# Other places in SBUF for the split weights where they are the stationary operand

## The chip, the cores and the metric

One core of a Trainium2 chip runs the whole program. The metric is the device time of one execution in microseconds; the time of before is the median of three runs.

## What is computed

Two decoder layers over 256 tokens of width 2048, float32. Layer 0 mixes tokens with block attention (16 heads of 128, one block of 256 tokens, so plain causal attention), layer 1 with retention (8 heads, keys of 256, values of 512). Behind each stands a gated feed-forward part with a causal convolution of width 3 (hidden width 5632), and every residual sum is followed by a layer norm. Cut to the two parts that carry most of the weights:

```python
qkv = jnp.einsum('bsd,de->bse', x, w_qkv)            # 2048 -> 3*2048, attention
# retention: w_q, w_k (2048 -> 2048), w_v, w_g (2048 -> 4096), w_o (4096 -> 2048)
def conv_ffn(x, w_in, conv_w, conv_b, w_out):
    u = jnp.einsum('bsd,df->bsf', x, w_in)           # 2048 -> 2*5632
    up = jnp.pad(u, ((0, 0), (CONV_WIDTH - 1, 0), (0, 0)))
    c = conv_b + up[:, 0:S] * conv_w[0]
    for j in range(1, CONV_WIDTH):
        c = c + up[:, j:j + S] * conv_w[j]
    g, val = jnp.split(c, 2, axis=-1)
    return jnp.einsum('bsf,fd->bsd', jax.nn.gelu(g) * val, w_out)
h = layer_norm(DEEPNORM_ALPHA * h + m, ln_g[i, 0], ln_b[i, 0])
```

## The kernel before

All weights, 478 MB, pass through the core once as 912 chunks. A chunk is 256 rows by 512 columns of a weight matrix: 128 partitions with CK = 2 row blocks of 512 float32 (COLS). There is a ring of RING = 4 slots. For each chunk SyncE loads `raw[:, s]` (512 KB), ScalarE rounds it into the high part `w_hi[:, s]` (float32r, `round_chunk`, recorded at L507), VectorE puts raw minus high into the low part `w_lo[:, s]` (`split_chunk`, L727), and TensorE multiplies. Each product of float32 values is made of three float32r products: high by high, high by low, low by high. The semaphores `hi_ready`, `lo_ready` and `products` hand a chunk on from engine to engine and a slot back; SyncE reloads `raw` of a slot once `lo_ready` says that the difference is made, ScalarE and VectorE overwrite the parts once `products` says that TensorE has finished with them. ScalarE and VectorE go through the chunks in `stream`, which takes other steps of a stage (`slots` ahead of a chunk, `behind` after it). `stream` for chunk s of a product prepares the chunk four further on, which for the last four belongs to the next product.

TensorE multiplies a chunk in one of three ways:
- token-major (`multiply_tile`, L272, L274, L275): 128x128 of the activations is stationary, a row block of 512 weight columns moves; the sum has tokens on the partitions. 12 matmuls a chunk. Used for values, gates and all output projections.
- feature-major narrow (`multiply` with `feature_major`, L289, L291, L293): 128x128 of the weights is stationary, 256 tokens of `x_hi` or `x_lo` move. 24 matmuls a chunk. Used for queries and keys.
- feature-major wide (`wide_multiply`, L330, L333): 128x128 of `w_hi` is stationary for 512 columns, the `x_hi` and `x_lo` of one row block side by side; then 128x128 of `w_lo` for the 256 columns of `x_hi`. 16 matmuls a chunk. Used for the input weights of the feed-forward part.

Every matmul loads its own stationary operand. The loads and matmuls of TensorE follow one another with no wait between them but that for `lo_ready` once a chunk. The order of stages is attention (narrow, narrow, token-major per group of four heads), its output, feed-forward 0 (wide, then token-major), retention (narrow, token-major, token-major per head), its output, feed-forward 1.

In SBUF each of h, x_parts, raw, w_hi and w_lo takes a multiple of 2048 bytes per partition, one after the other. Small tensors follow, and a padding "align" of 128 bytes, then arena (which holds the outputs of attention, retention and the hidden values, high and low, under other names) and side.

The lines that lay out the ring's parts are

```python
        raw = sb("raw", [P, RING, CK, COLS])
        w_hi = sb("w_hi", [P, RING, CK, COLS], F32R)
        w_lo = sb("w_lo", [P, RING, CK, COLS], F32R)
```

Of the kernel before, what the change touches and what calls it, by code (L numbers as in the profile page):

```python
# [22 lines left out]
F32 = mybir.dt.float32  # L23
# [12 lines left out]
CK = 2  # L36
RING = 4
# [22 lines left out]
HOLD = 2  # L60
AHEAD = 4
# [46 lines left out]
def build_trunk(nc, x, weights, attn_tab, causal, ident_in, ret_tab, decay_tab, conv_in, ln_g, ln_b, out):  # L108
    with ExitStack() as ctx:
# [11 lines left out]
        w_hi = sb("w_hi", [P, RING, CK, COLS], F32R)  # L121
        w_lo = sb("w_lo", [P, RING, CK, COLS], F32R)
# [55 lines left out]
        acc_a, acc_b, acc_c, mid = acc_ab[:, 0:2], acc_ab[:, 2:4], acc_cm[:, 0:2], acc_cm[:, 2:4]  # L178

# [85 lines left out]
        def _(pe):  # L265
            def multiply_tile(acc, t, s, xh, xl, kt, first):
# [3 lines left out]
                wh, wl = w_hi[:, s % RING], w_lo[:, s % RING]  # L270
# [234 lines left out]
        def _(act):  # L505
# [3 lines left out]
            def round_chunk(turn, s):  # L509
                act.wait_ge(raw_in[s], 16 * turn + 16)  # L510
                copy(w_hi[:, s], raw[:, s]).then_inc(hi_ready, 1)

            def stream(turn, chunks, slots={}, behind={}):


                for s in range(chunks):
# [4 lines left out]
                    round_chunk(turn + s // RING + 1, s % RING)  # L521
# [16 lines left out]
            for p in range(AHEAD):  # L538
                round_x(0, p)
                if p < RING:  # L540
                    round_chunk(0, p)
# [22 lines left out]
            def group(g):  # L564
                turn = Q_ATTN_LOOP + 3 * XQ * g
                stream(turn, XCH)
                stream(turn + XQ, XCH, {
# [16 lines left out]
            stream(Q_ATTN, XCH, behind=merged(x_slots(0), {1: [load_tables]}))  # L584
            with act.Fori(0, GROUPS - 1) as g:
                tail = group(g)
                stream(Q_ATTN_LOOP + 2 * XQ + 3 * XQ * g, XCH, tail)
            tail = group(GROUPS - 1)
# [3 lines left out]
            for n in range(1, NBLK):  # L592
                stream(Q_WO + n * XQ, XCH)
# [15 lines left out]
            def ffn(layer, q_in, n_in, nc_in, q_out, last):  # L609
# [25 lines left out]
                def behind_value(i):  # L635
# [3 lines left out]
                       behind=x_slots(2 * layer + 1))  # L639
                with act.Fori(0, FSTEPS - 1) as i:  # L640
                    turn = q_in + XQ + 2 * XQ * i
                    stream(turn, XCH, value_block(i))
                    stream(turn + XQ, XCH, merged(behind_value(i), {
                        XCH - 1: [lambda: conv_first_part(acc_ab)]}))
                stream(q_out - XQ, XCH, value_block(FSTEPS - 1))
# [5 lines left out]
                for i in range(NBLK // 2):  # L651
                    slots = merged(behind_value(FSTEPS - 1), {4: [load_behind_hidden]}) if i == 0 else {}

                    stream(q_out + OQ * i, 2 * HCH - (RING if last and i == NBLK // 2 - 1 else 0), slots)
# [20 lines left out]
            def retention_head(hd):  # L675
                turn = Q_RET_LOOP + 3 * XQ * hd
                stream(turn, XCH, {XCH - 1: [lambda: values_copy(rv_sb, acc_b, b_free)]})
                stream(turn + XQ, XCH, {XCH - 1: [make_gate]})
                return {1: [lambda: round_y(hd)]}

            stream(Q_RET, XCH, behind=merged(x_slots(2), {PIECES - AHEAD: [load_ret_tables]}))
            with act.Fori(0, RHEADS - 1) as hd:
                tail = retention_head(hd)
                stream(Q_RET_LOOP + 2 * XQ + 3 * XQ * hd, XCH, tail)
            tail = retention_head(RHEADS - 1)
            stream(Q_RWO, RCH, tail)
            load_ln_params(3)
            for n in range(1, NBLK):
                stream(Q_RWO + n * RQ, RCH)
# [34 lines left out]
        def _(dve):  # L724
            def split_chunk(turn, s):
                dve.wait_ge(hi_ready, RING * turn + (s + 1))
                dve.tensor_tensor(w_lo[:, s], raw[:, s], w_hi[:, s].bitcast(F32), ALU.subtract).then_inc(lo_ready, 1)  # L727

            def stream(turn, chunks, slots={}, at=0, behind={}):


                for s in range(chunks):
# [3 lines left out]
                    split_chunk(turn + (at + s) // RING + 1, (at + s) % RING)  # L736
# [9 lines left out]
            for p in range(AHEAD):  # L746
                low_x(0, p)
                if p < RING:
                    split_chunk(0, p)
# [47 lines left out]
            def group(g):  # L797
# [356 lines left out]
```

## Time and profile before

| | |
|---|---|
| median of 3 runs | 2656.99 us (2656.34 to 2658.08) |
| profiled execution | 2648.49 us |
| its span, first to last instruction | 2646.7 us |
| mean granted TensorE clock | 0.995 |
| busy: TensorE, its weight loads, VectorE, ScalarE, GpSimd | 2612.0, 2266.8, 1600.4, 1257.2, 15.2 us |

Times are microseconds from the start of the span, unless marked ns. PE is TensorE's matmuls, PEld its weight loads, DVE VectorE, ACT ScalarE, POOL GpSimd, SP SyncE. L12 is line 12 of the kernel. A matmul's record lasts from its start to the modelled end of its pipeline, so neighbours overlap; the pace is read from the starts. Some matmul records are missing from a trace. A float32 matmul (not float32r) has two records.

### The profile page before, as it was taken

Reading aid. Unit: us, or ns where it says so; the run is one execution under the profiler, and the core shown is the slowest. Engines: PE = TensorE matmul, PEld = TensorE weight load, DVE = VectorE, ACT = ScalarE, POOL = GpSimd, SP = SyncE. Lnnn points to the kernel's source line nnn. Section 1 sums busy time; section 2 is a strip of 40 time slices with the busy share of each in tenths; the row PEclk is TensorE's granted clock in tenths of the full one; section 3 lists DMA queues with packets and bytes.
Section 4 is the critical chain, followed back from the end, with each engine's and each line's share of the span. In section 5 each row is a group of like instructions: output and inputs, shape, how many; then the busy total and the mean of one; then the engine's idle time right before and its main releaser. Section 6 shows DMA issues by size and latency. Waiting matters only on the chain.

```text
span 2646.7 us, 40802 instructions
## 1 busy us (share of the span) xinstructions
PE 2612.0 (99%) x14368; PEld 2266.8 (86%) x14368; DVE 1600.4 (60%) x1842; ACT 1257.2 (48%) x1387; POOL 15.2 (1%) x38
## 2 busy tenths in 40 slices
PE   8999999999999999999999999999999999999998
PEld 8999888888888888888888888888788888888886
DVE  5666657666666654475555555554666666665455
ACT  4444435565656443334444444343365656554332
POOL 0000000000000000000000000000000000000000
PEclk9999999999999999999999999999999999999999
DMA  6545564555555565655555555566455555556654
GB/s 221 175 163 171 174 223 158 191 189 188 188 188 189 204 216 192 192 177 175 169 182 177 175 177 174 178 222 197 155 188 190 186 194 183 194 190 228 196 188 148
DMA packets 136978, 493.78 MB, mean 187 GB/s; under 512 B 15056, under 2 KB 17104, under 8 KB 135888
## 3 DMA queue, kind: packets, MB, share of 16 engines
q1 hardware_dynamic: 133136, 481.49, 55.1%
q10 hardware_dynamic: 3776, 11.37, 1.2%
q8 instruction: 46, 0.75, 0.1%
q14 instruction: 20, 0.16, 0.0%
HBM read 490.70 MB, written 2.10 MB: 186 GB/s over the span
## 4 chain that ended last, share of the span: by engine, by line
PE 98%; DVE 1%; DMA 0%; POOL 0%; issue 0%; ACT 0%; DVEq 0%; POOLq 0%; ACTq 0%
PE acc_ab L330 12%; PE acc_cm L330 12%; PE acc_ab L272 11%; PE acc_ab L274 11%; PE acc_ab L275 11%; PE acc_ab L333 6%; PE acc_cm L333 6%; PE acc_ab L289 5%; PE acc_ab L291 5%; PE acc_ab L293 5%; PE acc_cm L272 3%; PE acc_cm L275 3%; PE acc_cm L274 3%; PE acc_cm L356 1%; PE acc_cm L460 0%; DVE h L847 0%
## 5 line engine op out<-in xcount | busy, mean ns | idle before, releaser
L727 DVE TENSOR_TENSOR w_lo<-raw,w_hi 128x1024 fp32r<-128x1024 f32 x912 | 1105.8, 1223 | 838.2 <-ACT w_hi L507 835.2
L507 ACT ACTIVATE w_hi<-raw 128x1024 fp32r<-128x1024 f32 x912 | 948.7, 1055 | 882.7 <-PE acc_ab L275 469.7
L330 PE MATMUL acc_ab<-x_parts,w_hi 128*128 128x512 f32 x1408 | 493.7, 396 | 0.0
L330 PE MATMUL acc_cm<-x_parts,w_hi 128*128 128x512 f32 x1408 | 489.1, 394 | 0.0
L333 PE MATMUL acc_ab<-x_parts,w_lo 128*128 128x256 f32 x1408 | 391.4, 278 | 0.0
L333 PE MATMUL acc_cm<-x_parts,w_lo 128*128 128x256 f32 x1408 | 390.0, 277 | 0.0
L330 PEld LDWEIGHTS acc_ab<-x_parts,w_hi 128*128 128x128 f32 x1408 | 265.5, 189 | 61.3
L330 PEld LDWEIGHTS acc_cm<-x_parts,w_hi 128*128 128x128 f32 x1408 | 264.0, 188 | 61.3
L289 PE MATMUL acc_ab<-x_parts,w_hi 128*128 128x256 f32 x1024 | 295.8, 289 | 2.1 <-DVE w_lo L727 2.1
L291 PE MATMUL acc_ab<-x_parts,w_hi 128*128 128x256 f32 x1024 | 291.6, 285 | 0.0
L293 PE MATMUL acc_ab<-x_parts,w_lo 128*128 128x256 f32 x1024 | 291.6, 285 | 0.0
L272 PE MATMUL acc_ab<-w_hi,hid_hi 128*128 128x512 f32 x704 | 274.1, 389 | 0.0
L275 PE MATMUL acc_ab<-w_hi,hid_lo 128*128 128x512 f32 x704 | 273.9, 389 | 0.0
L274 PE MATMUL acc_ab<-w_lo,hid_hi 128*128 128x512 f32 x704 | 273.9, 389 | 0.0
L333 PEld LDWEIGHTS acc_ab<-x_parts,w_lo 128*128 128x128 f32 x1408 | 265.7, 189 | 0.0
L333 PEld LDWEIGHTS acc_cm<-x_parts,w_lo 128*128 128x128 f32 x1408 | 264.3, 188 | 0.0
L289 PEld LDWEIGHTS acc_ab<-x_parts,w_hi 128*128 128x128 f32 x1024 | 198.5, 194 | 2.9 <-issue 2.5
L291 PEld LDWEIGHTS acc_ab<-x_parts,w_hi 128*128 128x128 f32 x1024 | 198.5, 194 | 0.4
L293 PEld LDWEIGHTS acc_ab<-x_parts,w_lo 128*128 128x128 f32 x1024 | 198.3, 194 | 0.0
L272 PEld LDWEIGHTS acc_ab<-w_hi,hid_hi 128*128 128x128 f32 x704 | 132.1, 188 | 27.9 <-DVE w_lo L727 0.4
L274 PEld LDWEIGHTS acc_ab<-w_lo,hid_hi 128*128 128x128 f32 x704 | 132.1, 188 | 27.4
L275 PEld LDWEIGHTS acc_ab<-w_hi,hid_lo 128*128 128x128 f32 x704 | 132.1, 188 | 27.4
(111 smaller groups left out, 2839.2 us busy)
## 6 DMA issues: line engine op xcount, KB each, us to landing
raw<-in_weights_dram SPq DMA_DIRECT2D x912, 512.0 KB, 4.0
ln_gain<-in_ln_g_dram ACTq DMA_DIRECT2D x4, 1024.0 KB, 7.8
ln_bias<-in_ln_b_dram ACTq DMA_DIRECT2D x4, 1024.0 KB, 11.3
h<-in_x_dram SPq DMA_DIRECT2D x4, 512.0 KB, 8.4
decay_sb<-in_decay_tab_dram ACTq DMA_DIRECT2D x1, 1024.0 KB, 6.9
out_dram<-h SPq DMA_DIRECT2D x4, 256.0 KB, 2.5
out_dram<-h ACTq DMA_DIRECT2D x3, 256.0 KB, 2.5
conv_par<-in_conv_in_dram ACTq DMA_DIRECT2D x1, 352.0 KB, 11.4
```

Of the source, the lines that this page charges most:

```text
L272: pe.matmul(o, xh[:, kt + k, c], wh[:, k], start=first and k == 0, stop=False, skip_group_check=True)
L274: pe.matmul(o, xh[:, kt + k, c], wl[:, k], start=False, stop=False, skip_group_check=True)
L275: done = pe.matmul(o, xl[:, kt + k, c], wh[:, k], start=False, stop=True, skip_group_check=True)
L289: pe.matmul(o, wh[:, k, c], xh[:, kt + k, :], start=first and k == 0 and f % 2 == 0, stop=False, skip_group_check=True)
L291: pe.matmul(o, wh[:, k, c], xl[:, kt + k, :], start=False, stop=False, skip_group_check=True)
L293: last = pe.matmul(o, wl[:, k, c], xh[:, kt + k, :], start=False, stop=True, skip_group_check=True)
L330: pe.matmul(acc[:, f], w_hi[:, s % RING, k, c], x_parts[:, CK * s + k].rearrange("p a n -> p (a n)"), start=s == 0 and k == 0, stop=False, ...
L333: last = pe.matmul(acc[:, f, SEQ:2 * SEQ], w_lo[:, s % RING, k, c], x_hi[:, CK * s + k, :], start=False, stop=True, skip_group_check=True)
L356: last = pe.transpose(x_bank(p)[:, f, t * P:(t + 1) * P], h[:, t, p * PIECE + f * P:p * PIECE + (f + 1) * P], ident[:])
L507: return act.activation(o, i, ACT.Copy)
L727: dve.tensor_tensor(w_lo[:, s], raw[:, s], w_hi[:, s].bitcast(F32), ALU.subtract).then_inc(lo_ready, 1)
```

## The change

The parts of a slot get 64 floats more (256 bytes): `w_hi` and `w_lo` become [P, RING, SLOT] with SLOT = CHUNK + 64 and CHUNK = CK * COLS = 1024. A chunk's high and low part begin at a place within the slot: TOKENS = (0, 0) for the token-major products, FEATURES = (32, 48) floats for both feature-major ones, so at 128 bytes in w_hi and 192 bytes in w_lo. `parts(s, place)` makes the views. TensorE takes them by the kind of product, ScalarE and VectorE by two new arguments of `stream`: `place` for the chunks that belong to the running product and `then` for the four that belong to the next. Which values are computed, in which order and with which waits doesn't change. What lies behind w_hi in SBUF moves up by 1024 bytes, and what lies behind w_lo by 2048.

```diff
+CHUNK = CK * COLS
+TOKENS, FEATURES = (0, 0), (32, 48)
+SLOT = CHUNK + 64
...
-        w_hi = sb("w_hi", [P, RING, CK, COLS], F32R)
-        w_lo = sb("w_lo", [P, RING, CK, COLS], F32R)
+        w_hi = sb("w_hi", [P, RING, SLOT], F32R)
+        w_lo = sb("w_lo", [P, RING, SLOT], F32R)
...
+        def parts(s, place):
+
+            return [w[:, s, at:at + CHUNK].rearrange("p (k n) -> p k n", k=CK)
+                    for w, at in zip((w_hi, w_lo), place)]
...
-                wh, wl = w_hi[:, s % RING], w_lo[:, s % RING]
+                wh, wl = parts(s % RING, TOKENS)
...
-                wh, wl = w_hi[:, s % RING], w_lo[:, s % RING]
                 if feature_major:
+                    wh, wl = parts(s % RING, FEATURES)
...
+                wh, wl = parts(s % RING, FEATURES)
                 for k in range(CK):
                     for f in range(4):
                         c = slice(f * P, (f + 1) * P)
-                        pe.matmul(acc[:, f], w_hi[:, s % RING, k, c],
+                        pe.matmul(acc[:, f], wh[:, k, c],
                                   x_parts[:, CK * s + k].rearrange("p a n -> p (a n)"),
                                   start=s == 0 and k == 0, stop=False, skip_group_check=True)
-                        last = pe.matmul(acc[:, f, SEQ:2 * SEQ], w_lo[:, s % RING, k, c], x_hi[:, CK * s + k, :],
+                        last = pe.matmul(acc[:, f, SEQ:2 * SEQ], wl[:, k, c], x_hi[:, CK * s + k, :],
                                          start=False, stop=True, skip_group_check=True)
...
-            def round_chunk(turn, s):
+            def round_chunk(turn, s, place):
                 act.wait_ge(raw_in[s], 16 * turn + 16)
-                copy(w_hi[:, s], raw[:, s]).then_inc(hi_ready, 1)
-
-            def stream(turn, chunks, slots={}, behind={}):
+                copy(parts(s, place)[0], raw[:, s]).then_inc(hi_ready, 1)
+
+            def stream(turn, chunks, slots={}, behind={}, place=TOKENS, then=TOKENS):
...
-                    round_chunk(turn + s // RING + 1, s % RING)
+                    round_chunk(turn + s // RING + 1, s % RING, place if s + RING < chunks else then)
...
-            def split_chunk(turn, s):
+            def split_chunk(turn, s, place):
                 dve.wait_ge(hi_ready, RING * turn + (s + 1))
-                dve.tensor_tensor(w_lo[:, s], raw[:, s], w_hi[:, s].bitcast(F32), ALU.subtract).then_inc(lo_ready, 1)
+                wh, wl = parts(s, place)
+                dve.tensor_tensor(wl, raw[:, s], wh.bitcast(F32), ALU.subtract).then_inc(lo_ready, 1)
```

The rest of the diff hands `place` and `then` to each call of `stream`.

## Rows read from the trace of the kernel before

**Rows 1.** The page's busy time by engine, with share of the span and instructions.
```profile
PE 2612.0 (99%) x14368; PEld 2266.8 (86%) x14368; DVE 1600.4 (60%) x1842; ACT 1257.2 (48%) x1387; POOL 15.2 (1%) x38
```
**Rows 2.** The page's chain that ended last, share of the span by engine.
```profile
PE 98%; DVE 1%; DMA 0%; POOL 0%; issue 0%; ACT 0%; DVEq 0%; POOLq 0%; ACTq 0%
```
**Rows 3.** The waits of TensorE: who for whom, us in total, times, longest.
```profile
PE acc_cm L356 <- DVE h L855: 13.7, 6, 3.5
PE acc_cm L356 <- DMA h<-in_x_dram: 5.7, 1, 5.7
PE acc_ab L289 <- DVE w_lo L727: 2.1, 1, 2.1
PE acc_ab L272 <- DVE o_lo L794: 1.1, 1, 1.1
```
**Rows 4.** Timeline of a narrow product on TensorE: start, duration, instruction.
```profile
50.01 0.28 PE L293 MATMUL acc_ab<-x_parts,w_lo 128*128 128x256 f32 x1
...
51.09 0.28 PE L293 MATMUL acc_ab<-x_parts,w_lo 128*128 128x256 f32 x1
```
**Rows 5.** Timeline of a wide product on TensorE, f = 0 first.
```profile
500.51 0.39 PE L330 MATMUL acc_ab<-x_parts,w_hi 128*128 128x512 f32 x1
500.74 0.27 PE L333 MATMUL acc_ab<-x_parts,w_lo 128*128 128x256 f32 x1
500.85 0.40 PE L330 MATMUL acc_ab<-x_parts,w_hi 128*128 128x512 f32 x1
501.08 0.28 PE L333 MATMUL acc_ab<-x_parts,w_lo 128*128 128x256 f32 x1
501.20 0.39 PE L330 MATMUL acc_ab<-x_parts,w_hi 128*128 128x512 f32 x1
...
503.28 0.39 PE L330 MATMUL acc_ab<-x_parts,w_hi 128*128 128x512 f32 x1
...
506.06 0.39 PE L330 MATMUL acc_ab<-x_parts,w_hi 128*128 128x512 f32 x1
```
**Rows 6.** Timeline of a token-major product on TensorE.
```profile
999.90 0.39 PE L275 MATMUL acc_ab<-w_hi,hid_lo 128*128 128x512 f32 x1
...
1001.49 0.39 PE L272 MATMUL acc_ab<-w_hi,hid_hi 128*128 128x512 f32 x1
```
**Rows 7.** The page's groups: xcount | busy, mean ns | idle before.
```profile
L727 DVE TENSOR_TENSOR w_lo<-raw,w_hi 128x1024 fp32r<-128x1024 f32 x912 | 1105.8, 1223 | 838.2 <-ACT w_hi L507 835.2
L507 ACT ACTIVATE w_hi<-raw 128x1024 fp32r<-128x1024 f32 x912 | 948.7, 1055 | 882.7 <-PE acc_ab L275 469.7
L330 PE MATMUL acc_ab<-x_parts,w_hi 128*128 128x512 f32 x1408 | 493.7, 396 | 0.0
L289 PE MATMUL acc_ab<-x_parts,w_hi 128*128 128x256 f32 x1024 | 295.8, 289 | 2.1 <-DVE w_lo L727 2.1
L272 PE MATMUL acc_ab<-w_hi,hid_hi 128*128 128x512 f32 x704 | 274.1, 389 | 0.0
```
**Rows 8.** Stretches: length, busy by engine, clock, DMA share, GB/s.
```profile
8.00:50.00 42.00, 40.21 (x320) 40.24 (x321) 27.66 (x27) 19.14 (x23) 0.00 (x0) 1.00 0.68 236
430.00:890.00 460.00, 460.00 (x2655) 402.31 (x2654) 310.53 (x375) 275.11 (x313) 0.00 (x0) 1.00 0.57 189
900.00:1120.00 220.00, 220.00 (x971) 181.85 (x970) 112.42 (x104) 89.46 (x87) 0.00 (x0) 1.00 0.62 202
...
2400.00:2630.00 230.00, 230.00 (x1016) 190.39 (x1015) 116.26 (x108) 89.58 (x85) 0.00 (x0) 1.00 0.59 194
```
**Rows 9.** The chain in order of time around float32 products: start, us.
```profile
1199.94 0.86 PE acc_cm L468 x2
...
1227.33 0.87 PE acc_cm L478 x8
```
**Rows 10.** The wide 256-column matmuls, 500 to 560: ns min/median/max.
```profile
L333 PE MATMUL acc_cm<-x_parts,w_lo x66: 274/277/280, 500.0 to 544.8; 128*128 128x256 f32 x66
```
**Rows 11.** The page's DMA issues: KB each, us to landing.
```profile
raw<-in_weights_dram SPq DMA_DIRECT2D x912, 512.0 KB, 4.0
```

More of the change, by code:

```diff
@@ L540, in _ @@
                 if p < RING:
-                    round_chunk(0, p)
+                    round_chunk(0, p, FEATURES)
             def head_exp(g, i):
@@ L562, in head_round, with group @@
                 copy(o_hi[:, bass.ds(hd, 1), :], mid[:, 1:2, 0:SEQ]).then_inc(o_hi_done, 1)
-            def group(g):
+            def group(g, then):
                 turn = Q_ATTN_LOOP + 3 * XQ * g
-                stream(turn, XCH)
-                stream(turn + XQ, XCH, {
+                stream(turn, XCH, place=FEATURES, then=TOKENS)
+                stream(turn + XQ, XCH, then=then, slots={
                     3: [lambda: head_exp(g, 0)],
@@ L592, in _ @@
             for n in range(1, NBLK):
-                stream(Q_WO + n * XQ, XCH)
+                stream(Q_WO + n * XQ, XCH, then=FEATURES if n == NBLK - 1 else TOKENS)
             def conv_first_part(acc):
@@ L652, in ffn @@
                     slots = merged(behind_value(FSTEPS - 1), {4: [load_behind_hidden]}) if i == 0 else {}
-                    stream(q_out + OQ * i, 2 * HCH - (RING if last and i == NBLK // 2 - 1 else 0), slots)
+                    stream(q_out + OQ * i, 2 * HCH - (RING if last and i == NBLK // 2 - 1 else 0), slots,
+                           then=FEATURES if i == NBLK // 2 - 1 and not last else TOKENS)
             ffn(0, Q_FFN0, N_FFN0, NC_FFN0, Q_OUT0, False)
@@ L688, in _ @@
             for n in range(1, NBLK):
-                stream(Q_RWO + n * RQ, RCH)
+                stream(Q_RWO + n * RQ, RCH, then=FEATURES if n == NBLK - 1 else TOKENS)
             ffn(1, Q_FFN1, N_FFN1, NC_FFN1, Q_OUT1, True)
@@ L724, in _, with stream @@
         def _(dve):
-            def split_chunk(turn, s):
+            def split_chunk(turn, s, place):
                 dve.wait_ge(hi_ready, RING * turn + (s + 1))
-                dve.tensor_tensor(w_lo[:, s], raw[:, s], w_hi[:, s].bitcast(F32), ALU.subtract).then_inc(lo_ready, 1)
-            def stream(turn, chunks, slots={}, at=0, behind={}):
+                wh, wl = parts(s, place)
+                dve.tensor_tensor(wl, raw[:, s], wh.bitcast(F32), ALU.subtract).then_inc(lo_ready, 1)
+            def stream(turn, chunks, slots={}, at=0, behind={}, place=TOKENS, then=TOKENS, last=None):
                 for s in range(chunks):
@@ L735, in stream @@
                         step()
-                    split_chunk(turn + (at + s) // RING + 1, (at + s) % RING)
+                    split_chunk(turn + (at + s) // RING + 1, (at + s) % RING,
+                                place if s + RING < (last or chunks) else then)
                     for step in behind.get(s, ()):
@@ L795, in head_low, with group @@
                                   o_hi[:, bass.ds(hd, 1), :].bitcast(F32), ALU.subtract).then_inc(o_ready, 1)
-            def group(g):
+            def group(g, then):
                 turn = Q_ATTN_LOOP + 3 * XQ * g
                 stream(turn, XCH, {
-                    XCH - 1: [lambda: rotate(2 * g + 1, acc_b, b_free, g, k_t)]})
-                stream(turn + XQ, XCH, {
+                    XCH - 1: [lambda: rotate(2 * g + 1, acc_b, b_free, g, k_t)]}, place=FEATURES, then=TOKENS)
+                stream(turn + XQ, XCH, then=then, slots={
                     3: [lambda: head_max(g, 0)],
@@ L924, in _ @@
                     lambda: residual(1, n, (acc_a, acc_b)[n % 2], (a_free, b_free)[n % 2], N_WO + n // 2)]})
-            stream(Q_FFN0 - XQ, XCH - HOLD)
+            stream(Q_FFN0 - XQ, XCH - HOLD, last=XCH, then=FEATURES)
             layer_norm(1)
@@ L991, in ffn @@
                     else:
-                        stream(turn, HCH - (RING if last else HOLD), at=HCH)
+                        stream(turn, HCH - (RING if last else HOLD), at=HCH, last=HCH, then=TOKENS if last else FEATURES)
                 if last:
@@ L1053, in low_y, with retention_head @@
                                   ALU.subtract).then_inc(y_ready, 1)
-            def retention_head(hd):
+            def retention_head(hd, then):
                 turn = Q_RET_LOOP + 3 * XQ * hd
@@ L1074, in _ @@
                                      (N_RWO, NB_RWO)[n % 2] + n // 2)]})
-            stream(Q_FFN1 - RQ, RCH - HOLD)
+            stream(Q_FFN1 - RQ, RCH - HOLD, last=RCH, then=FEATURES)
             layer_norm(3)
```

59 lines of the change are left out of this document (30 added, 29 removed).

## The prediction, written before the changed kernel was run

> **What bounds the kernel now.** I read the engine table first, then the chain that ended last, then what TensorE waited for, and only then single matmuls. TensorE is busy 99% of the span, VectorE 60%, ScalarE 48% [rows 1]. The chain is 98% TensorE [rows 2], and all of TensorE's idle time is 22.6 us in nine waits, for the layer norms and the start [rows 3]. So nothing but the pace of the matmuls matters here, and a change that only moves operands can act on the path only through that pace.
>
> The pace comes from the distance between the starts of neighbouring matmuls; the durations in the group rows overlap and don't add up. Three kinds of product stream the chunks of weights:
> - narrow (L289, L291, L293), weights stationary, 256 moving columns: starts at 50.01 and 51.09 with nine steps between, 120.0 ns each [rows 4];
> - wide (L330, L333), weights stationary, a pair of 512 and 256 moving columns per place: 500.51 to 506.06 is 16 pairs (eight to a chunk, whose next chunk begins at 503.28), 346.9 ns a pair [rows 5];
> - token-major (L272, L274, L275), x, o, y or the hidden values stationary, 512 columns of weights moving: 999.90 to 1001.49 is seven steps, 227.1 ns each [rows 6].
>
> The counts are 1024 of each of three narrow lines (8 to a chunk, so 128 chunks) and 1408 in each of two accumulators for each wide line (2816 pairs, 352 chunks); of the 912 chunks 432 are left for the token-major products, 5184 matmuls at 12 each [rows 7]. Then 3072 x 120.0 = 369 us, 2816 x 346.9 = 977 us, 5184 x 227.1 = 1177 us: 2523 of the span of 2646.7. The rest is float32 products, transposes and the waits.
>
> Now the columns. The granted clock reads 1.00 in the stretches of every kind [rows 8], so a column takes 1/2.4 = 0.417 ns if one enters per cycle. 256 columns are 106.7 ns, and 13.3 are left over; a wide pair is 320.0, and 26.9 are left over, 13.4 for each of its two matmuls; 512 columns are 213.3, and 13.8 are left over. So **each matmul with its own load of 128 x 128 weights pays about 32 cycles extra**, whether it has 256 or 512 columns and whichever operand is stationary. That extra is the only thing this change can reach.
>
> Is it a fixed fee? The float32 products speak against. Two records of L468 with 512 columns take 0.86 us on the chain, 430 ns each: two cycles per column (426.7) and 3.3 left over. Eight transposes of 128 columns (L478) take 0.87: 108.8 ns each, two cycles per column (106.7) and 2.1 left over [rows 9]. They too load 128 x 128 float32 weights before each matmul. So a load every 109 ns can be nearly free when the moving operand is read at half the pace. That looks like two reads of SBUF in each other's way, which is what the place of an operand could change. It isn't proof: those records are another kind of pass.
>
> **Where the operands lie.** Before the change the rows of x_parts, raw, w_hi and w_lo take a multiple of 2048 bytes each. Between w_lo and arena lie 3968 bytes of small tensors (each at a multiple of 32) and the 128 of "align", together 4096. So the start of every operand of the three products has the same remainder modulo 512, and TensorE never ran them at another relative place. No row of before shows what 128 or 192 bytes do. There is one hint. Of the wide pairs the one with f even takes 0.34 us from start to start and the one with f odd 0.35, over and over; the 256-column matmul, which streams the same x_hi both times, takes 274 or 280 ns [rows 5, 10], where the weights stand 512 bytes further and the sum goes to the next PSUM bank. Between the starts it is 0.11 against 0.12. I read some 5 ns from it: the place of an operand can move a matmul by that much. The PSUM bank could be its cause as well.
>
> **The change part by part.**
> 1. Weights stationary, w_hi at 128 and w_lo at 192 bytes: 3072 narrow and 5632 wide loads, 8704 in all, on the path. Upper end of the gain: the extra falls from 13.4 to the 2.1 of the transposes, 11.3 x 8704 = 98 us. Lower end: nothing, and beyond it a loss, since a common start may just as well be the good place; doubling the extra would be 13.4 x 8704 = +117 us, which no row comes near. I take the size that the nearest row shows for an address, 5 ns a load, as a gain: 5 x 8704 = **43.5 us**. I choose the sign because the extra is at its full size everywhere while all operands share one start, and goes where reads are slower; a start at another place is then likelier to help than to hurt.
> 2. Weights moving: same places within a slot, but slots are 4352 bytes apart, so slot s starts 256 s further, modulo 1024. 5184 matmuls; slot 0 is as before. Cost nothing if 256 bytes don't matter; if they cost the same 5 ns in three slots of four, 5 x 3888 = 19 us either way. I take 0: in a wide chunk steps of 512 and 1024 bytes only trade 5 ns to and fro, and the two halves of the moving x_parts, 1024 bytes apart, both give 120 ns [rows 4].
> 3. ScalarE's copy and VectorE's difference write and read the shifted parts: the same 912 of each, 1055 and 1223 ns [rows 7]. No instruction or transfer is added or moved; SyncE's and ScalarE's queues are as before. A slower one is covered: in the wide stretch VectorE works 310.5 of 460 us and ScalarE 275.1 [rows 8], with 166 chunks in it; a chunk would need 0.9 us more VectorE time before it became late. Without that cover each microsecond per chunk in the 480 shifted chunks (128 narrow, 352 wide) would be on the path.
> 4. What is late next if the matmuls speed up: a wide chunk takes 2.775 us; all of the extra gone, 16 x 11.3 = 0.18 less, 2.59. Then 512 KB per chunk ask for 202 GB/s instead of 189. Another stretch moved 202 GB/s and the first 236, with TensorE busy throughout the one and nearly so in the other [rows 8]; the load lands after 4.0 us and three other slots cover it [rows 11]. So the gain is kept.
>
> The Trainium skill speaks against step 1. Its page "SBUF — State Buffer", section "Who interferes with whom", gives TensorE two independent read ports, for the moving operand and for the weights, and says TensorE never waits for anyone. By it the sum would be 0; the extra of 13.4 ns shows a fee that it doesn't name, and the trace can't tell whether that fee depends on the place. The same page, section "Specifications (TRN2)", gives lines of 16 bytes: a load's 512 bytes per partition are 32 lines, the number of extra cycles. If each line cost one cycle and the new places avoided it, the sum would be the upper end.
>
> Sum: 2646.7 - 43.5 = 2603.2 span, 2605.0 for the profiled execution (2648.5, 1.8 outside the span). That execution is 8.5 below the median of the runs, 2657.0, so the forecast is 2657.0 - 43.5 = **2613.5 us**.
>
> **The rivals.**
> - All of the extra goes: 2657 - 98 = 2559. For: 32 cycles are left at every place alike, and almost none in float32. Against: w_hi and w_lo get different shifts, while one stream is often a whole row of 2048 bytes, which sweeps every place of a smaller period whatever the start.
> - The place doesn't matter: 2657. For: the extra is the same 32 cycles for 256 and 512 columns and for either operand stationary, as a fixed fee of swapping weights would be; the 5 ns may be the PSUM bank. The two ports of the Trainium skill, as told above, would give the same.
> - The common start is the good one, and a shifted load meets the moving rows more often. Place: the same 8704 loads; price 5 ns each, +43.5, and up to 19 more in the token-major products: 2700 to 2720. It decides as soon as a narrow matmul takes over 120 ns. For: the padding "align" brings arena to the same remainder as w_hi, and there the pace is no worse than elsewhere. Against: nothing shows that pace to be below that of another start.
>
> **How the numbers follow.** Forecast, part of the extra goes (2585 to 2651): 0.45. All or nearly all goes (2556 to 2585): 0.14. No effect: 0.22. Slower: 0.19. A measurement of this kernel tells about 0.2% (5.3 us) from no change. Faster 0.59, same 0.22, slower 0.19. The range leaves out the slower case alone: 2557 to 2662.
>
> **What would show it.** Right: L289, L291 and L293 start less than 120 ns apart (115 for the forecast, 109 for all of it), wide pairs below 347 (337, 324), the token-major ones stay at 227, as do TensorE's waits of 22.6 us. If narrow and wide go different ways, the price per load is wrong, since I use one for both. If the token-major matmuls move, step 2 is wrong. If ScalarE or VectorE take the time back, TensorE waits for w_lo appear. If all starts are where they were, the fee is fixed.

## The result and the profile after

| | before | after |
|---|---|---|
| median | 2656.97 us (2656.34 to 2658.08, 4 executions) | 2640.66 us (2640.04 to 2642.14, 4 executions) |
| ratio, 95% interval | | 0.995 (0.9931 to 0.997) |
| profiled execution, its span | 2648.49, 2646.7 us | 2640.04, 2638.2 us |

The change makes the kernel 16.3 us (0.6%) faster in the medians. The forecast was 43.5 us. The profiled executions differ by 8.5 us only, and that difference between the two differences is half of the story. One execution of narrow_only further down had a mean granted clock of 0.556, where all others had 0.994 to 0.996; it took 4385 us and is left out of its row.

The page of after has, by engine and by chain, what [rows 1, 2] have for before:

```profile
PE 2603.5 (99%) x14368; PEld 2265.8 (86%) x14368; DVE 1600.7 (61%) x1842; ACT 1258.8 (48%) x1387; POOL 15.2 (1%) x38
PE 98%; DVE 1%; DMA 0%; POOL 0%; issue 0%; ACT 0%; DVEq 0%; POOLq 0%; ACTq 0%
```

Its waits of TensorE are the same nine as in [rows 3], 22.7 us against 22.6:

```profile
PE acc_cm L367 <- DVE h L869: 13.7, 6, 3.5
PE acc_cm L367 <- DMA h<-in_x_dram: 5.8, 1, 5.8
PE acc_ab L299 <- DVE w_lo L740: 2.1, 1, 2.1
PE acc_ab L282 <- DVE o_lo L808: 1.1, 1, 1.1
```

So the time went from the pace of the matmuls and from nothing else. The groups of VectorE and ScalarE, which write the shifted parts, hardly differ from [rows 7] (xcount | busy, mean ns | idle before):

```profile
L740 DVE TENSOR_TENSOR w_lo<-raw,w_hi 128x1024 fp32r<-128x1024 f32 x912 | 1106.1, 1223 | 832.2 <-ACT w_hi L518 823.7
L518 ACT ACTIVATE w_hi<-raw 128x1024 fp32r<-128x1024 f32 x912 | 950.1, 1057 | 874.3 <-PE acc_ab L285 468.9
```

Now the three kinds of product, in the timeline of TensorE (start, duration, instruction). First narrow, to hold against [rows 4]:

```profile
49.59 0.28 PE L303 MATMUL acc_ab<-x_parts,w_lo 128*128 128x256 f32 x1
...
50.99 0.28 PE L303 MATMUL acc_ab<-x_parts,w_lo 128*128 128x256 f32 x1
```

Twelve steps in 1.40 us: 116.7 ns each, where before had 120.0. Then wide, against [rows 5]:

```profile
500.47 0.39 PE L341 MATMUL acc_ab<-x_parts,w_hi 128*128 128x512 f32 x1
500.70 0.28 PE L344 MATMUL acc_ab<-x_parts,w_lo 128*128 128x256 f32 x1
500.81 0.39 PE L341 MATMUL acc_ab<-x_parts,w_hi 128*128 128x512 f32 x1
...
506.01 0.39 PE L341 MATMUL acc_ab<-x_parts,w_hi 128*128 128x512 f32 x1
```

Sixteen pairs in 5.54 us, 346.3 ns a pair; before had 346.9. Chunk by chunk it is the same number in both traces: the last matmuls of neighbouring wide chunks lie 2773 or 2774 ns apart in all 169 places of a layer where no other matmul lies between, in both layers, before and after. And token-major, against [rows 6]:

```profile
1000.09 0.39 PE L282 MATMUL acc_ab<-w_hi,hid_hi 128*128 128x512 f32 x1
...
1000.77 0.39 PE L282 MATMUL acc_ab<-w_hi,hid_hi 128*128 128x512 f32 x1
...
1001.45 0.39 PE L282 MATMUL acc_ab<-w_hi,hid_hi 128*128 128x512 f32 x1
```

Six steps in 1.36 us, 226.7 ns each: unchanged.

A steady chunk takes 2880, 2800, 2773.3 or 2720 ns here, and in cycles of 2.4 GHz (the granted clock is 1.00 in these windows) these figures turn out whole. A chunk of 24 narrow matmuls had 32.0 extra cycles per matmul before and has 24.0 after; a wide chunk of 16 has 32.0 in both; a token-major one of 12 has 32.0 in both. From here on I give the pace as **extra cycles per matmul**, the chunk's time times 2.4, less its columns, divided by its matmuls. They are taken from the starts of the last matmul of each chunk, the median over the chunks of a stage that hold no other matmul. At some places the chunks take turns between two or three lengths; the median then lies up to half a cycle off the mean (40.4 further down is 40.0 in the mean).

### The profile page after: what moved, and what is told of

Same layout as the page of the kernel before. It is cut to its first block, busy times and chain, and to the rows that moved or that the text cites. A ratio compares the mean times of both kernels' runs of the same rounds, so it can differ in the third digit from the quotient of the medians.

```text
span 2638.2 us, 40802 instructions
## 1 busy us (share of the span) xinstructions
PE 2603.5 (99%) x14368; PEld 2265.8 (86%) x14368; DVE 1600.7 (61%) x1842; ACT 1258.8 (48%) x1387; POOL 15.2 (1%) x38
## 4 chain that ended last, share of the span: by engine, by line
PE 98%; DVE 1%; DMA 0%; POOL 0%; issue 0%; ACT 0%; DVEq 0%; POOLq 0%; ACTq 0%
PE acc_ab L341 12%; PE acc_cm L341 12%; PE acc_ab L282 11%; PE acc_ab L284 11%; PE acc_ab L285 11%; PE acc_ab L344 6%; PE acc_cm L344 6%; PE acc_ab L299 5%; PE acc_ab L303 5%; PE acc_ab L301 5%; PE acc_cm L282 3%; PE acc_cm L285 3%; PE acc_cm L284 3%; PE acc_cm L367 1%; PE acc_cm L471 0%; DVE h L861 0%
## 5 line engine op out<-in xcount | busy, mean ns | idle before, releaser
L740 DVE TENSOR_TENSOR w_lo<-raw,w_hi 128x1024 fp32r<-128x1024 f32 x912 | 1106.1, 1223 | 832.2 <-ACT w_hi L518 823.7
L518 ACT ACTIVATE w_hi<-raw 128x1024 fp32r<-128x1024 f32 x912 | 950.1, 1057 | 874.3 <-PE acc_ab L285 468.9
L341 PEld LDWEIGHTS acc_ab<-x_parts,w_hi 128*128 128x128 f32 x1408 | 265.7, 189 | 57.9
L299 PE MATMUL acc_ab<-x_parts,w_hi 128*128 128x256 f32 x1024 | 293.1, 286 | 2.1 <-DVE w_lo L740 2.1
L301 PE MATMUL acc_ab<-x_parts,w_hi 128*128 128x256 f32 x1024 | 286.4, 280 | 0.0
L299 PEld LDWEIGHTS acc_ab<-x_parts,w_hi 128*128 128x128 f32 x1024 | 194.5, 190 | 2.9 <-issue 2.5
L301 PEld LDWEIGHTS acc_ab<-x_parts,w_hi 128*128 128x128 f32 x1024 | 194.7, 190 | 0.5
```

The lines of the kernel that those rows point to most:

```text
L299: pe.matmul(o, wh[:, k, c], xh[:, kt + k, :], start=first and k == 0 and f % 2 == 0, stop=False, skip_group_check=True)
L301: pe.matmul(o, wh[:, k, c], xl[:, kt + k, :], start=False, stop=False, skip_group_check=True)
L341: pe.matmul(acc[:, f], wh[:, k, c], x_parts[:, CK * s + k].rearrange("p a n -> p (a n)"), start=s == 0 and k == 0, stop=False, skip_group_ ...
L518: return act.activation(o, i, ACT.Copy)
L740: dve.tensor_tensor(wl, raw[:, s], wh.bitcast(F32), ALU.subtract).then_inc(lo_ready, 1)
```

## The experiments

The kernels of the scans give each stage its own places. For them the changed kernel was written so that `place` and `then` are handed down by stage, with one pair of floats each for the narrow, wide and token-major products of attention, retention and the two feed-forward layers. The other kernels of this section except after_again are written in the same way. Only the constants differ between them (x_moved has two lines more, shown there); those of scan4 are, in floats, with layer 0 and layer 1 in brackets:

```diff
-TOKENS, FEATURES = (0, 0), (32, 48)
+ATTN_NARROW, ATTN_TOKEN, FFN_WIDE, FFN_TOKEN = (16, 48), (48, 16), [(16, 32), (16, 48)], [(48, 32), (0, 8)]
+RET_NARROW, RET_TOKEN = (32, 0), (48, 48)
```

Places are given in bytes, w_hi first; "0 and 0" is the start of the slot. Nothing is left out of the computation in any of them.

### The changed kernel again, its slots alone, and its narrow half

after_again is the changed kernel. stride_only keeps the wider slots and begins all parts at their start:

```diff
-TOKENS, FEATURES = (0, 0), (32, 48)
+ATTN_NARROW, ATTN_TOKEN, FFN_WIDE, FFN_TOKEN = (0, 0), (0, 0), [(0, 0), (0, 0)], [(0, 0), (0, 0)]
+RET_NARROW, RET_TOKEN = (0, 0), (0, 0)
```

narrow_only keeps (32, 48) in the narrow products and (0, 0) in the wide ones:

```diff
-TOKENS, FEATURES = (0, 0), (32, 48)
+ATTN_NARROW, ATTN_TOKEN, FFN_WIDE, FFN_TOKEN = (32, 48), (0, 0), [(0, 0), (0, 0)], [(0, 0), (0, 0)]
+RET_NARROW, RET_TOKEN = (32, 48), (0, 0)
```

> The changed kernel once more, timed in five rounds beside the kernel before. In its trace the narrow matmuls start 116.7 ns apart instead of 120.0 and the wide pairs are as before, 346.7 ns. Theory A (the place of the stationary weights sets the pace of the narrow products alone): a chunk of 24 narrow matmuls takes 2.80 us instead of 2.88, over 128 chunks 10 us, so the median is 8 to 11 us below before and not 16. Theory B (the wide products gain too, which one profile hides): 15 to 18 us below before.

> Slots are 4352 bytes apart as in the changed kernel, and everything behind them lies where it lies there, but all parts begin at the start of their slots. Theory A: the pace of the narrow matmuls is 120.0 ns again and the time that of before within 1 us. Rival C (the slots' distance or the moved arena brings the gain, not the place within the slot): the narrow matmuls take 116.7 ns as in the changed kernel and the time is its time.

> 128 and 192 bytes in the narrow products alone; the wide ones have their parts at the start of the slots. Theory A: the time of the changed kernel within 1 us, narrow 116.7 ns. Theory B: 5 to 8 us slower than the changed kernel, wide pairs longer than in it.

| kernel | executions | median, lowest to highest | ratio to before, 95% |
|---|---|---|---|
| before | 24 | 2657.4 (2646.9 to 2667.8) | |
| after_again | 7 | 2641.4 (2640.7 to 2642.6) | 0.994 (0.9915 to 0.9965) |
| stride_only | 12 | 2657.0 (2647.7 to 2667.9) | 1.0002 (0.998 to 1.0024) |
| narrow_only | 11 | 2650.7 (2642.1 to 2659.5) | 0.9965 (0.9943 to 0.9986) |

The many executions of before show what three could not: its times don't spread, they fall into **three groups**. Timed beside the kernels of this section it ran 61 times: 19 lie between 2646.7 and 2648.9, 27 between 2656.0 and 2658.9 and 15 between 2665.2 and 2667.8. The changed kernel has one group, and after_again is 16.0 us below before: within theory B's 15 to 18, outside theory A's 8 to 11. Slots alone change nothing, so rival C is out: it is the place within the slot. And narrow_only sits between before and after, so theory A is out as well, though the trace of before and that of after have the same wide pace.

narrow_only is 9.3 us slower than the changed kernel, more than the 5 to 8 that theory B had. Two of its executions are at 2642, eight between 2647.8 and 2652.1, one at 2659.5. Its profiled execution, of the eight, shows that the narrow gain isn't certain either: the steady narrow chunks of attention take 2880 ns in it, as in before, and those of retention 2800.

The trace of stride_only shows what the groups are. It is an execution of the middle group, and its wide stages run at two paces. Layer 0, then layer 1:

```profile
499.93 0.40 PE L342 MATMUL acc_cm<-x_parts,w_hi 128*128 128x512 f32 x1
...
502.75 0.40 PE L342 MATMUL acc_ab<-x_parts,w_hi 128*128 128x512 f32 x1
...
2000.55 0.39 PE L342 MATMUL acc_cm<-x_parts,w_hi 128*128 128x512 f32 x1
...
2003.33 0.39 PE L342 MATMUL acc_cm<-x_parts,w_hi 128*128 128x512 f32 x1
```

Eight pairs take 2.82 us in layer 0 and 2.78 in layer 1; over whole stages the mean chunk is 2826.7 and 2773.3 ns, 40 and 32 extra cycles. The counts of matmuls in two windows of wide products say the same. The columns are the window, its length, TensorE's busy time and matmuls, clock, DMA share and GB/s. In stride_only the first window has fewer:

```profile
430.00:890.00 460.00, 460.00 (x2606) 1.00 0.55 186
1925.00:2390.00 465.00, 465.00 (x2689) 1.00 0.56 189
```

In narrow_only, whose profiled execution took 2652.1 us, it is the second:

```profile
430.00:890.00 460.00, 460.00 (x2656) 1.00 0.56 189
1925.00:2390.00 465.00, 465.00 (x2634) 1.00 0.55 185
```

Each has one stage at the slow pace, and a stage keeps its pace through all its 176 chunks. 53.4 ns times 176 is 9.4 us, the distance between the groups. The granted clock reads 1.00 in all four lines, so it is not the clock.

### The wide half

wide_only has (32, 48) in the wide products and (0, 0) in the narrow ones:

```diff
-TOKENS, FEATURES = (0, 0), (32, 48)
+ATTN_NARROW, ATTN_TOKEN, FFN_WIDE, FFN_TOKEN = (0, 0), (0, 0), [(32, 48), (32, 48)], [(0, 0), (0, 0)]
+RET_NARROW, RET_TOKEN = (0, 0), (0, 0)
```

> 128 and 192 bytes in the wide products alone; the narrow ones begin at the start of the slots. The runs of the kernel before fall into three clusters, near 2647, 2657 and 2667 us; a wide stage of 176 chunks ran at 2773 ns a chunk or, in other executions, at 2827, 53.5 ns more, which is 9.4 us a stage. Theory B2 (the shift in the wide products takes away the slow way of running, and leaves the fast one as it is): all executions near 2647 us, none near 2657 or 2667, wide chunks at 2773 ns in both layers. Rival (the shift does nothing for the wide products, and the tight times of the changed kernel are luck or come from the narrow products before them): the executions spread over 2647, 2657 and 2667 as before.

Measured: twelve executions, all between 2647.0 and 2649.0 us, median 2647.8, beside 17 of before in its three groups (6, 6 and 5); ratio 0.9967 (0.9947 to 0.9987). Narrow chunks 2880 ns, wide 2773.3 in both layers. That is theory B2: in the wide products the shift gains nothing against the good pace, and takes the bad pace away. Counted by the groups of times, 57 of 122 wide stages of before were slow (no slow one of before itself was profiled; stride_only and narrow_only show the pace). If slow and good stages were equally likely and independent, twelve executions without one would have a chance of a half to the 24th power. The other kernels with 128 and 192 in the wide products have one group too: 4 executions of after, 7 of after_again, 6 of narrow_64_192.

### The map of places

Two points for each of narrow and wide, and up to four for token-major, come out of one profile. Each scan was executed once: 2683.5, 2673.9, 2672.9, 2677.4, 2685.5, 2667.7, 2650.5 and 2639.1 us for scan1 to scan8.

> A look at other places, one pair of w_hi and w_lo shifts per kind of product, in bytes: attention narrow 128 and 128, retention narrow 0 and 64, wide 64 and 64 in layer 0 and 128 and 128 in layer 1, token-major (weights moving) 128 and 192 in attention, 0 and 128 in retention, 128 and 128 in feed-forward 0, 64 and 64 in feed-forward 1. Theory A1 (the shift of each load against the moving rows decides for itself): the narrow matmuls of attention are faster than 120 ns on two lines of three, those of retention on one. Theory A2 (the difference between w_hi and w_lo decides, since the reads of one load run into the next): attention narrow 120.0, retention narrow below it. For both, wide pairs stay near 347 ns, and the token-major ones leave 227 ns if the relation of the two operands matters there too.

> Shifts in bytes for w_hi and w_lo: attention narrow 0 and 128, retention narrow 0 and 192, wide 0 and 64 in layer 0 and 0 and 128 in layer 1, token-major 0 and 64 in attention, 64 and 0 in retention, 0 and 192 in feed-forward 0, 64 and 128 in feed-forward 1. So far in extra cycles per narrow matmul: both at 0 gives 32, 0 and 64 gives 26.7, 128 and 128 gives 29 to 32, 128 and 192 gives 24. Theory D (the difference between the two shifts decides, 64 bytes being good): narrow 0 and 128 near 32, 0 and 192 no better than 32; token-major 64 and 128 better than 64 and 64, which gave 37.4. Rival S (each load's own shift decides, and costs add): narrow 0 and 192 is 32 less what 192 brings in w_lo, so at or below 32, and at 24 if w_lo carries the whole gain.

> Attention narrow 64 and 0, retention narrow 64 and 128, wide 0 and 192 in layer 0 and 64 and 0 in layer 1, token-major 64 and 192 in attention, 128 and 64 in retention, 128 and 0 in feed-forward 0, 192 and 0 in feed-forward 1. Theory D: narrow 64 and 128 is 24 to 27 extra cycles, narrow 64 and 0 above 29. Rival S: narrow 64 and 128 follows from the other points as a sum of a part for w_hi and a part for w_lo. Either way the token-major products stay at or above 32, the figure with both at 0.

> Attention narrow 64 and 192, retention narrow 128 and 0, wide 64 and 128 in layer 0 and 64 and 192 in layer 1, token-major 192 and 64 in attention, 192 and 192 in retention, 192 and 128 in feed-forward 0, 0 and 32 in feed-forward 1. Theory D: narrow 64 and 192 near 32, wide 64 and 128 at 32 like 128 and 192. Rival S: wide 64 and 128 at 40, since 64 and 64 gave 40 in w_hi's larger loads. Token-major at or above 32.

> Attention narrow 192 and 0, retention narrow 192 and 64, wide 128 and 0 in layer 0 and 128 and 64 in layer 1. Token-major by less than 64 bytes: 16 and 16 in attention, 240 and 240 in retention, 32 and 32 in feed-forward 0, 0 and 16 in feed-forward 1. Theory G (what counts is how the reads of loads and of moving rows fall among 64-byte places, in the order of the loads, not a sum and not a difference): the narrow points differ, none below 16; wide stay at 32 or above. For token-major, small shifts cost less than the 64-byte ones, which cost 5 to 19 extra cycles. Rival (steps of 64 bytes are what the places are made of): a shift of 16 bytes costs nothing in the token-major products.

> Attention narrow 192 and 192, retention narrow 192 and 128, wide 192 and 0 in layer 0 and 192 and 64 in layer 1; token-major 0 and 240 in feed-forward 0, 224 and 0 in feed-forward 1, the rest as before or 128 and 128. Theory G: narrow points between 16 and 32 extra cycles, wide at 32 to 40, token-major above 32. A wide point under 32 would show that the floor of the wide products isn't one full cycle for each 16 bytes of weights.

> Around the good narrow place of 64 and 192: 96 and 192 in attention, 64 and 224 in retention; wide 192 and 128 in layer 0 and 192 and 192 in layer 1. Theory G with places of 64 bytes: half a place away the gain is partly lost, 16 to 28 extra cycles. Rival (a sharp coincidence of single lines): at 32 bytes off it is gone, 28 to 32.

> Neighbours of the good places: narrow 128 and 64 in attention and 32 and 192 in retention; wide 224 and 0 in layer 0 and 192 and 32 in layer 1. Theory G: between 16 and 32 extra cycles in the narrow products, and the wide ones lose part of the 8 cycles that 192 and 0 gained, 24 to 40. Rival (the floor lies at another place): one of them is below 16 or 24.

Extra cycles per matmul, with the runs above for 0 and 0 and for 128 and 192. Rows are the place of w_hi, columns that of w_lo. Two numbers are two paces seen at one place.

Narrow:

| w_hi | w_lo 0 | 64 | 128 | 192 |
|---|---|---|---|---|
| 0 | 32 | 26.7 | 30.0 | 26.3 |
| 64 | 26.7 | not run | 27.8 | **16** |
| 128 | 28.0 | 26.7 | 29.2, 32 | 24, 32 |
| 192 | 26.7 | 29.3 | 21.3 | 26.7 |

Wide:

| w_hi | w_lo 0 | 64 | 128 | 192 |
|---|---|---|---|---|
| 0 | 32, 40 | 32 | 36 | 32 |
| 64 | 40 | 40 | 36 | 40 |
| 128 | 38.6 | 32 | 37 | 32 |
| 192 | **24** | 40 | 32 | 40.4 |

Off the grid, narrow has 26.7 at 96 and 192 and at 32 and 192, and 24.6 at 64 and 224; wide has 29.3 at 224 and 0 and 32 at 192 and 32.

Token-major, where the weights move: 32 at 0 and 0 and more at every other place that was run, on the grid from 37.4 (0 and 192, 64 and 64, 128 and 0) over 40 to 46 (0 and 64, 64 and 128, 64 and 192, 128 and 128, 128 and 192, 192 and 64, 192 and 128) to 48 or more (64 and 0, 192 and 192, 192 and 0 with 50.6). Two places of the grid have two paces, 0 and 128 with 42.7 and 48, 128 and 64 with 37.4 and 45.2. 16 bytes are enough to spoil it: 44 at 16 and 16, 44.6 at 0 and 16. So are 32 bytes (44 at 0 and 32, 48 at 32 and 32), and from the other side 52 at 0 and 240, 48 at 224 and 0, and 48 or 56 at 240 and 240.

What the expectations were worth: theory D (the difference decides) fell on the narrow row 64 and 192 with 16 cycles, where the same difference at 0 and 128 gives 30. Rival S (a part for each of the two that add) fell with it: moving w_lo from 0 to 192 gains 5.7 cycles where w_hi is at 0, 10.7 where it is at 64 and nothing where it is at 192. What stands is theory G in its weak form, that both places count together, in the order in which the loads come; it names no value ahead, and I have no model that does. The wide place of 192 and 0, under the 32 that I had taken for the floor, was forecast by no theory. Three smaller expectations failed as well: scan1 had the wide pairs stay near 347 ns, where they took 353.3 (64 and 64) and 351 (128 and 128); scan2 had token-major 64 and 128 better than 64 and 64, and it was worse (45.4 against 37.4); scan5 had shifts of 16 and 32 bytes cost the token-major products less than those of 64, and they cost 12 to 24 cycles. Half a grid step away the gain of the good narrow place is mostly lost (26.7, 26.7 and 24.6), as are 5 of the 8 cycles of the good wide one at 224 and 0, and all 8 at 192 and 32.

### Is it the relation of the two operands, or the place of the weights?

x_moved leaves all parts at the start of their slots and moves x_parts by 64 bytes, and all that lies behind by 256:

```diff
+        sb("ahead", [P, 16])
         x_parts = sb("x_parts", [P, KT, 2, SEQ], F32R)
+        sb("behind", [P, 48])
```

> All parts begin at the start of their slots, but x_parts lies 64 bytes further and everything behind it 256 bytes further. Relative to the moving x the stationary weights are then at -64, which is 192 modulo 256, for both parts. Theory R (only the relation of the two operands counts, modulo 256 bytes): narrow matmuls at 26.7 extra cycles as with shifts of 192 and 192 in scan6, wide ones at 40 as with 192 and 192 in scan7, token-major ones with x stationary at 48 as with 192 and 192 in scan4, those with arena stationary at 32. Rival (the place of the weights in SBUF counts by itself, for instance against the writes of ScalarE and VectorE): narrow 32, wide 32 or 40, token-major 32 everywhere, as in the kernel before.

The timeline of x_moved, narrow, wide, token-major with x stationary, token-major with the hidden values (in arena) stationary:

```profile
49.99 0.28 PE L306 MATMUL acc_ab<-x_parts,w_lo 128*128 128x256 f32 x1
...
52.82 0.28 PE L306 MATMUL acc_ab<-x_parts,w_lo 128*128 128x256 f32 x1
...
500.33 0.40 PE L344 MATMUL acc_ab<-x_parts,w_hi 128*128 128x512 f32 x1
...
503.16 0.39 PE L344 MATMUL acc_ab<-x_parts,w_hi 128*128 128x512 f32 x1
...
79.84 0.39 PE L285 MATMUL acc_cm<-w_hi,x_parts 128*128 128x512 f32 x1
...
82.64 0.39 PE L285 MATMUL acc_cm<-w_hi,x_parts 128*128 128x512 f32 x1
...
999.88 0.39 PE L285 MATMUL acc_ab<-w_hi,hid_hi 128*128 128x512 f32 x1
...
1002.60 0.39 PE L285 MATMUL acc_ab<-w_hi,hid_hi 128*128 128x512 f32 x1
```

24 narrow steps in 2.83 us, eight wide pairs in 2.83, twelve token-major steps in 2.80 and twelve in 2.72. By chunks: 26.7, 40.4, 48 and 32 extra cycles. The first three are the numbers that the map has for 192 and 192, the fourth is that of 0 and 0, where both operands kept their relation. The parts that ScalarE and VectorE write lay, modulo 256 bytes, where they lie in the kernel before, so their place by itself doesn't set the pace. Nor do the writes of these two engines: in the wide products between 460 and 900 us the mean step behind a 512-column and behind a 256-column matmul is 226.7 and 113.3 ns in both_best while both engines work and 226.6 and 113.4 while neither does, and in the slow stage of stride_only 236.4 and 117.0 against 236.3 and 117.0. So theory R holds: **the relation of the stationary to the moving operand, modulo 256 bytes, moves the pace**. It was tried at one displacement, 64 bytes. The wide number alone would prove nothing, since 40 is also the slow pace at 0 and 0; the narrow 26.7 and the 48 beside 32 in the token-major products carry it. The relation alone doesn't fix the pace, since some places have two.

### Better places

narrow_64_192 takes the good place for the narrow products, and both_best, of which this is the edit, that for the wide ones too:

```diff
-TOKENS, FEATURES = (0, 0), (32, 48)
+ATTN_NARROW, ATTN_TOKEN, FFN_WIDE, FFN_TOKEN = (16, 48), (0, 0), [(48, 0), (48, 0)], [(0, 0), (0, 0)]
+RET_NARROW, RET_TOKEN = (16, 48), (0, 0)
```

> The changed kernel with 64 and 192 bytes in the narrow products (as in attention of scan4, where a narrow matmul had 16 extra cycles, 113.3 ns) and 128 and 192 in the wide ones. Theory A+B2: a narrow chunk takes 2720 ns instead of the changed kernel's 2800, 80 ns over 128 chunks is 10.2 us, so 2631 us, all executions within 2 us since the wide stages keep their one way of running. Rival (narrow products fall into a slower way of running at these places too, as one run of the shifted kernels showed for all of attention): 2633 to 2641, spread over the executions.

> 64 and 192 bytes in the narrow products and 192 and 0 in the wide ones, where a chunk took 2720 ns in scan6 instead of 2773. Theory A: 53.3 ns less over 352 wide chunks is 18.8 us off the 2631.2 of narrow_64_192, so 2612.4. Rival (the gain of the wide products at 192 and 0 holds in some executions only, as the pace of 2773 does in the kernel before): several clusters of times between 2612 and 2640.

| kernel | executions | median, lowest to highest | ratio to before, 95% |
|---|---|---|---|
| narrow_64_192 | 6 | 2631.2 (2629.9 to 2632.4) | 0.9902 (0.9873 to 0.993) |
| both_best | 5 | 2612.1 (2611.1 to 2612.6) | 0.9829 (0.9806 to 0.9852) |

Both came out within 0.4 us of what the map said. both_best beats the kernel before by 1.7% and the changed one by 1.1% (2612.1 against 2641.4). Its timeline, 24 narrow matmuls and eight wide pairs:

```profile
49.98 0.28 PE L300 MATMUL acc_ab<-x_parts,w_hi 128*128 128x256 f32 x1
...
52.70 0.28 PE L300 MATMUL acc_ab<-x_parts,w_hi 128*128 128x256 f32 x1
...
500.09 0.39 PE L342 MATMUL acc_ab<-x_parts,w_hi 128*128 128x512 f32 x1
...
502.81 0.39 PE L342 MATMUL acc_ab<-x_parts,w_hi 128*128 128x512 f32 x1
```

2.72 us for either: 113.3 ns a narrow matmul, 340.0 a wide pair. Nothing took the gain back: TensorE waits nine times in it too, 23.2 us, though the weights now flow at 193 and 196 GB/s in the wide windows:

```profile
430.00:890.00 460.00, 460.00 (x2698) 1.00 0.59 193
1925.00:2390.00 465.00, 465.00 (x2691) 1.00 0.59 196
```

## Why the prediction was wrong

The sign and the range held, and so did the mechanism in outline: the place of the stationary operand against the moving one moves the pace. The price of a load in it was wrong: 43.5 us forecast and 16.3 measured.

- **Step 1, the price of a load, is the step that failed.** I took 5 ns for each of 8704 loads, narrow and wide alike. Measured on steady chunks: narrow 3.3 ns (8 cycles), wide nothing against the pace that the trace of before showed. Narrow and wide went different ways, which the prediction had named as the sign of a wrong price. The 5 ns came from the even and odd wide pairs in [rows 5, 10]. In the trace of after that alternation is gone (every wide 256-column matmul of that timeline lasts 0.28 us, whether f is even or odd) and the chunk is as long as before, so it showed how a fixed sum was shared between neighbours, not a price. In before the steps behind the 512 and the 256 columns average 231.7 and 115.0 ns, in after 229.6 and 117.1: another split of the same 346.7.
- **The same step for the narrow products, by size.** 3.3 ns times 3072 would be 10.2 us. The narrow stages gave 7.8 of the 8.5 us between the two spans: summed over their chunks (from TensorE's first instruction on), attention went from 207.9 to 205.2 us, retention from 202.5 to 197.4. The rest of the 10.2 is lost in products that float32 transposes or head products cut into; there most narrow matmuls still run at 120.0 ns, as in this row pair of after, twelve steps in 1.44 us:

```profile
1161.11 0.28 PE L301 MATMUL acc_ab<-x_parts,w_hi 128*128 128x256 f32 x1
...
1162.55 0.28 PE L301 MATMUL acc_ab<-x_parts,w_hi 128*128 128x256 f32 x1
```

- **A term that was not in the sum.** The slow pace of wide stages costs 9.4 us a stage, and by the groups of times 57 of 122 stages had it, 8.8 us an execution on average; the change takes it away. I had the sign of it before me: the profiled execution was 8.5 us below the median of runs that agree within 1.8 us. I carried that distance through as an offset. It was one slow wide stage, by the groups of times, which the runs had and the trace had not. The trace of before was a trace of its best group.
- Both together: 9.4 us for the slow stage and 6.4 for the narrow products (wide_only's 2647.8 against after_again's 2641.4) make 15.8; the medians of before and after_again, 2657.4 and 2641.4, are 16.0 apart. The spans had given 8.5 us for the narrow products and what goes with them; that gain varies between executions, as nine chunks of attention's first two products show, which ran at 2800 ns in the trace of after and at 2880 in that of after_again (0.7 us).
- **The sign was luck in part.** Its ground was that a start at another place is likelier to help than to hurt. That is so for the narrow products, where the common start is the slowest place. For the wide ones nine of the fifteen other places of the map cost 4 to 8 cycles more than the good pace at 0 and 0, five cost the same and one gains; 8 cycles over 5632 loads are 18.8 us, more than the 10.2 that the narrow ones could give. 128 and 192 is one of the five.
- **"Is it a fixed fee?"** was answered rightly: the extra can go down, to 16 cycles in the narrow and 24 in the wide products. Whether the float32 products of [rows 9] are cheap for the same reason no run tested. That nearly all of it can go, the first rival, was not seen at any place run.
- **No effect**, the second rival, was wrong. Shifting x_parts by 64 bytes costs a token-major matmul with x stationary 16 cycles, 226.7 to 233.3 ns. The page "SBUF — State Buffer" of the Trainium skill, section "Who interferes with whom", has two independent read ports for TensorE and says that it never waits on anyone. The runs don't agree: with all else in place the pace depends on where the two operands lie. Where the two reads meet, no run here shows.
- **The slower rival** named the right danger for the wrong products. The common start is the best place found for the token-major ones, where every shift costs 5 to 24 cycles. For the wide ones it is one of the better places while they keep its good pace, and for the narrow ones it is the worst.
- **Step 2** (slots 256 bytes further cost nothing) held: 1.0002 for stride_only. **Step 3** held: 1057 and 1223 ns against 1055 and 1223. **Step 4** held, even for the larger gain of both_best.

What stays open: what decides, at the start of a wide stage, which of its two paces it takes. It holds for a whole stage and differs between executions of one kernel, and other places remove it; no run here changed the start of a stage. The traces do show where a pace is chosen. In none of the 17 traces does it change for good inside an unbroken row of chunks of one kind; it changes where float32 matmuls or another kind of product stand between, in either direction. In the retention of scan1 the token-major chunks (0 and 128) go from 2773 to 2800 ns across the float32 matmuls of the scores and back to 2773 across the next ones, head after head. A wide stage has float32 transposes among its first seven chunks alone, and then 169 chunks with none. Open too is a rule that gives the map's numbers ahead. And that the second pace never occurs in both_best rests on five executions and two profiled stages.

## What to carry to other kernels

Where a matmul kernel is bound by back-to-back matmuls with a new stationary operand each, compare the distance of starts with the columns: what is left over per load may depend on where the stationary operand lies against the moving one, and a few dozen padded bytes, chosen per kind of product, can move it. Scan such places with a different value in each stage of one kernel, since the stages give independent readings in one profile, and add up the steady chunks before timing the best. And if the profiled execution lies off the median of tight runs, ask what that execution had or lacked before carrying the distance through as a constant.

## What the runs showed of the hardware that was not expected

- What a float32r matmul of 256 or 512 columns with its own load of 128 x 128 weights pays beyond its columns hangs on where its two operands lie. With both at one remainder modulo 256 bytes it is 32.0 cycles on average over a steady chunk (40 in the slow wide stages); at best 16.0 in a stream of 256-column matmuls (narrow_64_192) and 24.0 where 512 and 256 columns alternate (both_best); up to 56 at 240 and 240 with the weights moving (scan5).
- The relation of the operands works modulo 256 bytes (in stride_only the slots begin at 0, 256, 512 and 768, and the token-major chunks take 2720 ns in all four), and down to 16 bytes: a moving operand 16 bytes off costs 12 more cycles, 32 to 44 (scan5).
- The same stream of instructions over the same places has more than one steady pace, kept for 176 chunks: 2773.3 and 2826.7 ns a wide chunk at 0 and 0, 2800 and 2880 ns a narrow chunk at 128 and 192 (after and narrow_only). The pace changes only across float32 matmuls or a change of the kind of product, to the slower one or to the faster.
